# A two-block model kernel: order of the first projection, the pooling sums and a weight split spread over the scan, and group norm in batches

## What is computed

```python
def rwkv_pool_mixer(h, w_in, mu, ...):
    y = h @ w_in                                  # 18 tiles of 128 features
    ys = y[..., :SHIFT_WIDTH]                     # 14 of them, mixed with the step before
    ys = ys + (prev - ys) * mu
    r, k, v, wd, ad, gd = jnp.split(ys, RWKV_SPLITS, axis=-1)
    decay = jnp.exp(-jnp.exp(wlog))               # from tanh(wd) @ w_up
    a = jax.nn.sigmoid(a0 + ad @ a_up)
    g = jax.nn.sigmoid(gd) @ g_up
    kk = kk / jnp.maximum(jnp.linalg.norm(kk, axis=-1, keepdims=True), 1e-12)
    kf = kf * (1.0 + (a - 1.0) * k_a)
    o = rwkv7_scan(rf, dec, kf, vf, kk, a_h)      # a recurrence over time
    mean = jnp.mean(o, axis=-1, keepdims=True)    # group norm over each head of 64
    var = jnp.mean(jnp.square(o - mean), axis=-1, keepdims=True)
    o = ((o - mean) * lax.rsqrt(var + GN_EPS)).reshape(B, L, RWKV_WIDTH) * ln_w + ln_b
    o = (o + bonus) * g
    ...                                           # diffs: running means over 2, 4, 8, 16 steps minus u
    z = jnp.einsum('blgc,gcd->blgd', d, pool_w) * pool_scale
    return jnp.concatenate([o, z], axis=-1) @ w_out
```

## Time and profile before

| what | value |
|---|---|
| median of 3 runs | 2733.13 us (2727.08 to 2738.0) |
| the profiled execution | 2738.7 us, of it 2736.9 us in the span |
| PE busy | 2445.6 us (89%) |
| DVE, ACT, POOL busy | 1424.1, 1035.3, 434.5 us (52%, 38%, 16%) |
| granted TensorE clock, mean | 0.911 |

### The profile page before, as it was taken

The page is one execution under the profiler, slowest core; times in us unless marked ns, Lnnn a source line. Parts: engine busy times, 40 slices in busy tenths (PEclk is TensorE's granted clock), DMA queues, the critical chain, the costliest instruction groups (busy, mean ns, idle before and its releaser), DMA issues. The chain is left out here.

```text
span 2736.9 us, 41459 instructions
## 1 busy us (share of the span) xinstructions
PE 2445.6 (89%) x16564; PEld 1737.2 (63%) x16564; DVE 1424.1 (52%) x2207; ACT 1035.3 (38%) x1793; POOL 434.5 (16%) x550
## 2 busy tenths in 40 slices
PE   6779778999997999868999999978978998899998
PEld 5668656888875666546544585655655786754445
DVE  3762456652254434446653259464443535578833
ACT  4423324222233433324332336436653444433322
POOL 0236433001232000024001230104322000000000
PEclk9987878999998998679999999998887999999999
DMA  3130001322221011001323212101101231122222
GB/s 150 47 94 1 1 31 62 124 93 93 94 79 47 24 47 62 31 1 64 123 93 122 93 63 93 62 24 47 39 16 66 98 131 62 63 93 92 95 95 74
DMA packets 38649, 190.94 MB, mean 70 GB/s; under 512 B 12144, under 2 KB 14448, under 8 KB 17464
## 3 DMA queue, kind: packets, MB, share of 16 engines
q1 hardware_dynamic: 37944, 186.44, 19.1%
q10 hardware_dynamic: 512, 1.85, 0.2%
HBM read 185.08 MB, written 3.19 MB: 69 GB/s over the span
## 5 line engine op out<-in xcount | busy, mean ns | idle before, releaser
L452 DVE SCALAR_TENSOR_TENSOR wsp<-raw_w,wsp 128x2048 f16<-128x2048 f32 (+2 forms) x180 | 399.8, 2221 | 199.2 <-ACT wsp L432 191.0
L415 PE MATMUL ps<-hn,wsp 128*128 128x512 f16 x1968 | 433.4, 382 | 5.7 <-DVEq L239 4.7
L410 PE MATMUL ps<-hn,wsp 128*128 128x256 f16 (+1 forms) x2976 | 361.3, 285 | 45.3 <-DVEq L239 15.2
L432 ACT ACTIVATE wsp<-raw_w 128x2048 f16<-128x2048 f32 (+2 forms) x180 | 327.0, 1817 | 113.7 <-PE ps L413 48.2
L410 PEld LDWEIGHTS ps<-hn,wsp 128*128 128x128 f16 x2976 | 300.5, 102 | 103.3 <-POOL hn L877 16.4
L415 PE MATMUL ps<-big,wsp 128*128 128x512 f16 (+1 forms) x1740 | 350.4, 363 | 6.5 <-DVEq L239 6.5
L413 PE MATMUL ps<-hn,wsp 128*128 128x264 f16 x2880 | 344.7, 283 | 7.3 <-DVE hn L703 7.3
L415 PEld LDWEIGHTS ps<-hn,wsp 128*128 128x128 f16 x1968 | 193.1, 98 | 235.7 <-issue 5.7
L413 PEld LDWEIGHTS ps<-hn,wsp 128*128 128x128 f16 x2880 | 289.0, 101 | 59.2 <-issue 8.6
L415 PEld LDWEIGHTS ps<-big,wsp 128*128 128x128 f16 x1740 | 173.7, 100 | 173.5 <-issue 21.0
L410 PE MATMUL ps<-big,wsp 128*128 128x256 f16 (+1 forms) x1800 | 207.9, 278 | 6.0 <-DVE big L403 4.4
(11 more groups left out here) (395 smaller groups left out, 3095.2 us busy)
## 6 DMA issues: line engine op xcount, KB each, us to landing
raw_w<-slabs SPq DMA_DIRECT2D x162, 1024.0 KB, 5.1
raw_w<-slabs SPq DMA_DIRECT2D x10, 512.0 KB, 5.4
raw_w<-slabs SPq DMA_DIRECT2D x8, 384.0 KB, 5.0
h<-xin SPq DMA_DIRECT2D x1, 2112.0 KB, 7.8
out<-hn SPq DMA_DIRECT2D x8, 256.0 KB, 2.1
big<-memx ACTq DMA_DIRECT2D x1, 1024.0 KB, 4.8
sml<-small SPq DMA_DIRECT2D x1, 768.0 KB, 10.6
cst<-consts SPq DMA_DIRECT2D x1, 710.0 KB, 8.9
```

The costliest lines, as they stand in the source:

```text
L410: mm = L.eng.matmul(ps[:rows, b, 0:T // 2], lhsT, rhs[:, z, :], start=first, stop=last)
L415: mm = L.eng.matmul(two(ps[:rows, b, 0:T]), lhsT, rhs, start=first, stop=last)
L432: L.fin(L.eng.activation(wsp[:, n % NW, 0, lo:hi], raw_w[:, q % 2, 0:hi - lo], ACT.Copy, scale=WSCALE), "hi")
L452: L.fin(L.eng.scalar_tensor_tensor(wsp[:, n % NW, 1, lo:hi], raw_w[:, q % 2, 0:hi - lo], WSCALE, wsp[:, n % NW, 0, lo:hi], ALU.mult, ALU.s ...
```

## The change

1. **Order of projection 1.** The keys (tiles 4 to 7) come straight behind tile 12, gd (tile 13) and r later. All that hangs on them moves one place earlier: the decays behind p=1, a behind p=2, sums of squared keys behind p=2 to 5, g behind p=7 to 10, Grams behind p=9 and 10. On VectorE `kk_norm` and `decayed` stand between p=3 and p=6 and the first `elem` ahead of the mixing of p=6. On GpSimd the four products with a come ahead of the four with r.
2. **SP's queue.** The round trip of the inverses stands behind the loads of slab 5 and no longer behind those of slab 6.
3. **Pooling sums.** The same 14 pieces and four endings, but never two in one gap between chunks.
4. **A weight split** (one slab, two halves) moves from behind the scan into it, behind chunks 9 and 12.
5. **Group norm in batches.** Four means, four squares, then the sums of all eight heads into one 88x48 block, one root and one reciprocal for all of them, which ScalarE widens and TensorE spreads. ln_w, ln_b, the bonus and g follow on VectorE in three instructions a tile; ScalarE makes the high part.
6. **The pooling part** is split into high and low by GpSimd and comes first in the output projection (the weight's rows are rolled by 4 tiles on the host).

```diff
-EV_ORDER = [12, 13] + list(range(4, 8)) + list(range(4)) + list(range(8, 12)) + list(range(14, 18))
+EV_ORDER = [12] + list(range(4, 8)) + [13] + list(range(4)) + list(range(8, 12)) + list(range(14, 18))
...
     TensorE, projection 1
-                if p == 2:
+                if p == 1:
                     L.take("tg")
                     for j in range(4):
                         low_rank(slice(0, 64), 0, 12, j)
-                if p in (10, 11):
+                if p in (9, 10):
                     pe.wait_ge(sem("elem"), 1)
-                    grams_pe(p - 10)
+                    grams_pe(p - 9)
...
     SyncE
-                if n == 6:
+                if n == 5:
                     sp.wait_ge(sem("elem"), 4)
...
     VectorE, projection 1
             for p in range(18):
+                if p == 5:
+                    L.take("ecum1", 2)
+                    decayed(0)
+                    kk_norm(L, 2)
+                if p == 6:
+                    decayed(1)
+                    kk_norm(L, 3)
+                    decayed(2)
+                    decayed(3)
+                    L.tell("elem")
                 if p < 14:
                     shift_mix(p, sc[:, 0, :])
...
+                if p in (3, 4):
+                    kk_norm(L, p - 3)
...
     VectorE and ScalarE, end of a chunk of the scan
+                if c in (9, 12):
+                    split_lo_part(L, dcnt)      # split_hi_part(L, cnt) on ScalarE
...
     TensorE, group norm
+            for j in range(4):
+                b = acc_open(L, cnt)
+                L.put(mm_T(L, b, bones, X[1][:, j, :], T0, True, True), "acc_full")
+            for j in range(4):
+                L.take("sqg")
+                for b in range(6):
+                    mm = pe.matmul(gn_sums(b, j), squares[j][:, b * 88:(b + 1) * 88], bones[:, 0:P:64],
+                                   start=True, stop=True)
+            L.put(mm, "gsum")
+            pooled(0)
+            pooled(1)
+            for j in range(4):
+                L.take("gwide")
+                st_open(L, cnt)
+                for b in range(6):
+                    at = (b % 3) * 88
+                    mm = pe.matmul(ps[:, 6 + b // 3, at:at + 88],
+                                   gn_wide(j)[0:88, b, :], ident[0:88, 0:88], start=True, stop=True)
+                L.put(mm, "st_full")
+                if j < 2:
+                    pooled(2 + j)
...
     ScalarE, group norm
+            for j in range(4):
+                evac(L, cnt, T0, lambda v: act.activation(halves(knorm[:, j, :], T0), v, ACT.Copy, scale=-1.0 / 64))
+            for j in range(4):
+                L.take("cen")
+                L.fin(act.activation(squares[j], X[1][:, j, :], ACT.Square), "sqg")
+            L.take("gsum")
+            L.fin(act.activation(gn_roots[0:88, :], ps[0:88, 7, 0:48], ACT.Sqrt, bias=eps_gn[0:88, :],
+                                 scale=1.0 / 64), "wide_root")
+            pooled_act(0)
+            pooled_act(1)
+            L.take("cen")
+            for j in range(4):
+                if j == 2:
+                    pooled_act(2)
+                    pooled_act(3)
+                L.fin(act.copy(gn_wide(j)[0:88, :, :].rearrange("p b (h c) -> p b h c", h=2),
+                               gn_rinv[0:88, :, 2 * j:2 * j + 2].unsqueeze(3).to_broadcast([88, 6, 2, 64])), "gwide")
+            for j in range(4):
+                L.take("scaled")
+                L.fin(act.copy(hl(X[1][:, j, :])[0], two(sc[:, j % 2, 0:T0])), "rounded")
...
     GpSimd, scan
             for c in range(2, NCH):
                 widened(c)
                 blocks_of(c)
-                g, i = divmod(c - 2, 4)
-                if g < 4 and i <= g:
-                    window(g, i)
-            window(3, 3)
+                at = c - 2
+                for g in range(4):
+                    if 0 <= at < g + 2:
+                        window(g, at)
+                    at -= g + 2
```

163 lines of the change are left out of this document (90 added, 73 removed).

## The result

The changed kernel takes 2718.36 us (median of 20 executions, 2704.69 to 2734.64), the kernel before 2737.0 beside it (20 executions): a ratio of 0.9945, 95% interval 0.9924 to 0.9966. That is 18.6 us less, where 44 were forecast. The profiled execution took 2733.96 us, 16 above the median, so three more profiles of the same kernel stand in the table further down.

What follows compares the result with a forecast made beforehand. It took PE to be held by waits for `elem`, inverses and GpSimd, by its clock, and by group norm's three-engine chain. 0 - 10 - 12 - 22 = -44 on 2738.7 gives 2694.7, 5.6 above the median: 2689, range 2671 to 2711.

Steps and rivals of the forecast that it cites:

- (a): Scan rival: the clock falls inside the scan; one half-clock stretch gives 2697, two 2708; chance 0.28.
- (c): Projection 1 rival: longer new waits, `elem` 4 to 8 later; 2693 to 2700 alone, up to 2712 with (a); chance 0.10.
- Projection 1, forecast 0: Reorder of projection 1: three new waits of 14 us replace waits of 18.5; cost 0, bounds -5 and +4.
- p=11 ends at 147.5: Projection 1 on PE: tile p=11 ends at 147.5, now 148.87, so inverting starts at 159.0.
- 6.6, 3.9 and 3.5: Projection 1: PE's new waits ahead of the decays' products, the fourth key sum and the first product with g.
- Round trip, forecast -10: Inverses between projection 1 and scan: sent at 184.3, not 189.6, 3.9 out and acknowledged; -10 us, bounds -5 and -12.
- do not decide, by 1 us: Ahead of the scan: VectorE's split, products and masks give PE first values at 194, ahead of the inverses at 195.3.
- Scan, forecast -12: Scan: last mark 95.0 us behind the first, against 106.9; -12 us, bounds -15 and 0.
- if PE's clock holds at waits of under 2.98: Scan: condition on the -12; the wait of 2.98 for GpSimd had been followed by 24 us at 0.51.
- The walk through GpSimd's gaps: Scan, chunk by chunk: GpSimd needs 5.25 with a piece, 6.9 with an ending; endings cost 0.7, 1.9, 1.9, 1.1, pieces 0.2.
- The forecast's size of a split half: Scan: each weight split half costs PE some 2.7 us, twice, partly in the shadow of an ending.
- Group norm, forecast -22: Group norm to first output projection evacuation: 40 us instead of 61, and 1 for the split; -22, bounds -18 and -26.

Runs made afterwards that it cites:

- e13: Changed kernel with projection 1 in old order, split behind the scan, at most one GpSimd piece per gap, three endings behind the scan, fillers 18 and 24: median 2673.3 us.
- e14: e13 with projection 1 in the new order and 36 fillers ahead of the scan instead of 18: median 2692.5 us.
- e6: The kernel before, with only the inverses sent ahead of the two weight slabs: median 2731.8 us.
- e5: The changed kernel with projection 1 back in its old order on every engine: median 2706.8 us.
- e17: The changed kernel run again with nothing edited, one profiled execution: 2712.2 us.
- e12: e7 with the two split halves back behind chunks 9 and 12 of the scan: median 2721.0 us.
- e7: The changed kernel with the weight split behind the scan, GpSimd's windows spread by its room and three endings behind the scan: median 2699.1 us.
- e15: e13 with no filler matmul anywhere: median 2687.8 us.
- e9: e8 with projection 1 in its old order: median 2698.9 us.
- e2: The changed kernel with both halves of the weight split put back behind the scan: median 2716.6 us.
- e8: e7 plus filler matmuls on constants, in PE's waits ahead of the scan and in the group norm: median 2693.3 us.
- e10: e8 with 28 and 24 more filler matmuls in two waits of projection 1: median 2697.6 us.
- e16: e14 with VectorE's mixing of p=4 ahead of the split and first two key norms: 2686.5 us, one execution.

## Why the prediction was wrong, step by step

The sign held (18.6 us faster, above the 13.7 that can be told), the size did not: the median is 29 above the forecast and 7 above the range. The pair of rivals (a) and (c), for which I had allowed up to 2712, is what came.

**Projection 1, forecast 0, measured +11.5 on the median.** The step that failed is the end of the tile p=11 on PE, from which the inverting was worked out: "p=11 ends at 147.5". The path was right: VectorE mixes that tile as soon as it is evacuated and has 11.0 us of work behind it (forecast 10.7). But the tile ended at 154.6, so the inverting started at 166.51 and not at 159.0. The waits are not to blame: they came to 6.30, 5.58 and 1.36 where 6.6, 3.9 and 3.5 were forecast. Two terms are. By its start the tile was 3.1 late, since gd was mixed at 120.3 and not at 116.9: VectorE got p=3 1.1 later (91.26, forecast 90.2; PE's tile behind the decays' products took 8.03 and not 7.29), and its instructions were slower than the rows they were taken from (a split 5.08 and not 4.62, the first half of a mixing 1.57 and not 0.71), with GpSimd at work in the same 6 us. The other 4.0 came inside the tile: a stand of 2.29 that no row of before shows, and half clock for a part of what was left. VectorE's idling was not missed, the forecast had it idle until 90.2. Over all profiles the start differs by 5.7 us on the mean between the orders; what the medians show beyond that (11.5, and 19.2 between e13 and e14) no run attributes. Rival (c) had the effect (later by 4 to 8; the start of the inverting was 7.5 late) by another mechanism: it had longer waits.

**Round trip, forecast -10.** The mechanism held: sent within 0.1 us, 11.4 from the last inverting instruction to PE's first inverse matmul (203.38; forecast 11.0). Counted from the last inverting instruction it took 20.8 before, so the term was 9.4 at its place. Alone it was worth 4.9 on the median, and where the rest went stays open. One step was wrong without costing much: VectorE's split, products and masks "do not decide, by 1 us". They do, in e6 too, but the first inverse product came only 0.4 later for it.

**Scan, forecast -12.** In place of 95.0 it took 103 to 123 in four profiles. On the median the term is about -6, as a remainder: e5 has all parts but projection 1 and is 29.9 below its kernel before; less 4.9 and 18.9 this leaves 6.1, if the parts add, which the scan's experiments make doubtful. The step that failed is the condition I wrote behind the sum, "if PE's clock holds at waits of under 2.98". It does not: stretches of some 20 us at half clock followed waits of 1.82, of 0.80, and of 1.14 with 2.20. Rival (a) was the right mechanism with too small a price: I gave it one or two stretches of 8 and it had three or four. The walk through GpSimd's gaps itself was near: waits of 0.80, 1.82 and 0.80 where 0.7, 1.9 and 1.9 were forecast (1.69 for the third in e17, where the clock was up), and in e13 5.3 per chunk with a piece in each gap. The forecast's size of a split half, 2.7, counts the waits alone; e12 against e7 gives 22 for two.

**Group norm, forecast -22.** 18.9 on the median alone; in the profiles the stretch went from 61.0 to 41.05. First evacuation 41.05 behind the scan's last copy, forecast 40. The sums took 5.36 for 48 records (forecast 7.1); the table load of 1.28 ahead of the root was not in the sum.

**The sum.** +11.5 - 4.9 - 18.9 - 6.1 = -18.4, against -18.6 measured. That it closes proves nothing, since the 6.1 is the remainder of the same medians. By it the forecast of -44 lost 11.5 to projection 1, 5 to the round trip, 6 to the scan and 3 to the group norm. In the profiles the shares are others: the scan was 16.5 us longer than before and not 12 shorter, which is the larger miss there.

## What to carry to other kernels

Before moving work between stages, follow the chain back from the instruction that releases the next stage, through every engine, and write down at each link which engine the other waits for. Neither the sum of one engine's waits nor another engine's backlog at some early time gives the end: here the chain went from PE to VectorE, back to PE and to VectorE again, and PE lost its time at half clock and in a stand, not in its waits. Where matmuls are small and many, price a wait not by its length but by what the clock may do behind it: here a wait of 1.8 us was followed by over 20 us at half clock, so spread side work until no gap exceeds the pace (a piece of 1.41 in every gap but no ending of 3.07), and take the median of many executions, since one profile of such a stretch may be 20 us off. Two disturbances that bring the clock down do not add, and neither do their cures: here each alone was worth -3 to 2 us and both together 19. Where a wait can't be removed, harmless matmuls in it kept the clock higher (group norm 5.9 us shorter in e13 than in e15), but too many of them delay the real work (e9).

## What the runs showed of the hardware that was not expected

- Waits of equal length for GpSimd were followed by different clocks: 1.82 us by 24 us at 0.50 (changed kernel, 242.32), 1.69 by some 3 us (e17, 266.42), 1.78 by none (e2, 267.45, at 1.00 over the next 8 us); 2.70 by 6 us in e8 and over 20 in e9. The Trainium skill (TensorE: Matmul & The Clock Gate, "A second HAM failure mode: psum-queue depth-cycling") describes a clock that swings between its two levels because PE micro-idles between groups of matmuls. The swinging is what the trace shows (0.50 and 1.00 in one scan); no run here shows what decides between a short and a long stretch.
- PE stood for 0.76 to 2.29 us with no releaser in the profile, in all 13 profiles with the new order of projection 1. By the trace's records it is always behind the 986th matmul from the start: 14 matmuls into the tile p=11 in twelve profiles, and in e10, which has 52 fillers ahead of it, 52 matmuls earlier, inside the Gram products. So it seems to hang on the place in PE's stream of instructions and not on what stands there. It was shortest behind the longest waits for VectorE and ScalarE (0.76 in e16 after 13.90, 1.38 in e10 after 4.38, else 1.62 to 2.29 after 1.36 to 2.04). In the four profiles in which it was 2.00 or longer the rest of the tile ran in part at half clock (5.67), in the others with the same 34 matmuls it took 4.00. In the seven profiles with the old order the 986th record falls inside the second Gram products, some 10 us behind the long wait for `elem`, and there is no such stand. What it is stays open; no run tried to move it.
